# Three more gate/up blocks by seven products, and 22 sums of w_down quarters made by transfers in DRAM

## The chip, the cores and the metric

One core of a Trainium2 chip runs the whole kernel. The metric is the device time in microseconds, the median of the runs. TensorE (PE) multiplies, VectorE (DVE) and ScalarE (ACT) prepare operands and take results, SyncE (SP) issues most transfers, GpSimd (POOL) issues a few and computes some square roots.

## The reference

One layer on x of 512 tokens by 1024 columns, in float32. Everything up to the second residual sum stays as it is; what matters here is its last part, with a hidden width of 2816, that is 22 blocks of 128 columns:

```
h = rms_norm(x, ffn_norm)
a, b = jnp.split(h @ w_gate_up, 2, axis=-1)      # 1024 x (2*2816)
x = x + (jax.nn.silu(a) * b) @ w_down            # 2816 x 1024
return rms_norm(x, final_norm)
```

## The kernel before

**Two-part arithmetic.** A float32 product is made of three products in the format float32r. Each operand is split into a high part (a cast on ACT, "hi") and a low part (source minus high part, a subtraction on DVE, "lo"). So each tile of weights costs PE three matmuls, ACT one cast and DVE one subtraction. The order is counted by semaphores: w_hi and w_lo count split weight parts, used counts the parts that PE is done with. Each engine works its list in the written order.

**Stages.** norm, front, pair (four head pairs), mix, rounds (ten), out, ffn_first, ffn_head, turns, ffn_last, down. The last four make the feed-forward part. Blocks 0 to 3 belong to ffn_first and ffn_head. The fifteen turns (v = 0 to 14) make blocks 4 to 18, each gate and up block by a Strassen-like scheme with seven products of half size: the parts F11, F21, F2, F1, F3, F22, F4 (lines 367 to 370), each 12 matmuls 256 columns wide (`turn_product`, L1346 to L1350). DVE forms four sums of weight quarters per turn (`turn_sums`, `turn_last_sum`), subtracts low parts (`turn_lo`, L2823), adds bank results (`turn_post`, L2831) and multiplies gate with up (`turn_hidden`, L2839). The stage ffn_last makes blocks 19 to 21 plainly: 48 matmuls of 512 columns per block (`whole`, L913 to L917), with `scaled` on DVE and `silu` on ACT.

**Hidden tiles.** Two blocks make one tile r (0 to 10). `hid_sum(r)` is three DVE instructions (L2709, L2714, L2717), then `hidden_hi` (ACT, L1832) and `hid_low` (DVE, L2723) split it. SUMMED is the order in which tiles come. In ffn_last tiles 0, 1, 9 and 10 are handled.

**down.** The product with w_down is also a seven-product scheme in four passes over the eleven tiles: PE's units are two times three matmuls of 512 columns (`both`, `times`, L1400 to L1402). Pass 1 takes two units per tile, from parts NU + 2r and NU + 2r + 1, where NU is the number of parts before this stage. Part NU + 2r is a quarter of w_down as loaded; part NU + 2r + 1 is a sum of two quarters, made on DVE by `first_sum` (L2676) into chain(r). Pass 2 takes three units per tile, with two more sums (`second_sums`, L2926, L2927). Split parts live in a ring of nine places. `down_hi(r)` and `down_lo(r)` or `parts_lo` (L2668) fill it. The high parts of the tile for pass 2 come from `second_hi` (ACT, L1848) and `second_lo` (DVE, L2888). ACT loads another activation table (L1979) between `down_hi(2)` and `down_hi(3)`.

**Transfers.** SP loads 256 KB pieces into `raw`, a store with three slots, each load held back by a wait on w_lo. In ffn_last it also brings back the four 512 KB pages of the second residual (x2_kept, L777), which DVE adds to after pass 1. POOL issues 16 small transfers in the stage pair (L880, L882), and its next work is a square root near 436 us.

Of the kernel before, what the change touches and what calls it, by code (L numbers as in the profile page):

```python
# [36 lines left out]
          ("ffn_first", 1, 2), ("ffn_head", 1, 6), ("turns", 1, 105),  # L37
          ("ffn_last", 1, 6), ("down", 1, 77)]
# [7 lines left out]
TURNS = range(4, 19)  # L46
PER_TURN = 7
TURN_LOADS = 2 * len(TURNS)
LAST_STAGES = ("ffn_last", "down")
# [4 lines left out]
    "free0": dict(front=1, pair=2, mix=1, out=4, ffn_head=1, ffn_last=1),  # L54
    "free1": dict(front=1, pair=2, mix=1, out=3, ffn_first=1, ffn_head=1, ffn_last=1),
    "free2": dict(front=1, pair=1, mix=1, out=4, ffn_head=1, ffn_last=1),
    "free3": dict(front=1, pair=5, mix=1, out=4, ffn_head=1, ffn_last=1),
    "free4": dict(front=2, pair=4, mix=2, out=2, ffn_head=1, ffn_last=1),
    "free5": dict(front=3, pair=4, mix=1, out=2, ffn_head=1, ffn_last=1),
# [20 lines left out]
    "vector_step": dict(norm=11, front=23, pair=5, mix=6, rounds=8, ffn_first=3, ffn_head=5, turns=7, ffn_last=4,  # L80
# [40 lines left out]
def hybrid_block(nc, x, attn_norm, w_in, b_forget, b_gate, w_proj_attn, pool_w, pool_scale,  # L121
# [26 lines left out]
    with ExitStack() as ctx:  # L148
# [36 lines left out]
        w_sums = nc.dram_tensor("w_sums", [16 * P, D // 2], F32, kind="Internal").ap()  # L185
        x2_kept = nc.dram_tensor("x2_kept", [S, D], F32, kind="Internal").ap()
# [125 lines left out]
        def chain(r, n=1):  # L312

            if r == 0:
                return DIAG
            if r < 3:
                return flat[:, (r - 1) * S:(r - 1 + n) * S]
            return early_32[:, (r - 3) * S:(r - 3 + n) * S]

        def in_one(u, n):  # L320

            at = (u - NU) % RING
            if n == 2 and at in (2 * SLOTS - 1, RING - 1):
                return ((0, 1), (1, 1))
            return ((0, n),)

        def ring_part(buf, u, n=1):

            at = (u - NU) % RING * S
            if at >= 2 * SLOTS * S:  # L330
                at += (2 if buf is whi else 5) * S
                return operands[:, at:at + n * S]
            return buf[:].rearrange("p s c -> p (s c)")[:, at:at + n * S]
# [42 lines left out]
        SUMMED = list(TILES.values()) + [0, 1, 9, 10]  # L376
# [116 lines left out]

        def down_raw(k, half, n=1):
# [62 lines left out]
        out_summed, sums_kept = sem("out_summed"), sem("sums_kept")  # L557
        mix_summed, mix_hi, mix_lo = sem("mix_summed"), sem("mix_hi"), sem("mix_lo")
# [32 lines left out]
        def _(sp):  # L591
            def load(stage, i, j, halves, width=P):
# [7 lines left out]
                elif stage == "ffn_last" and j < SLOTS:  # L600
                    v, part, sums = ((-2, F22, 3), (-1, F21, 4), (-1, F22, 4))[j]
                    v += len(TURNS)
                    sp.wait_ge(w_lo, turn_part(v, part) + 1)
                    sp.wait_ge(turn_summed, 4 * v + sums)
                    sp.sem_inc(loads_begun, 1)
# [5 lines left out]
                for src, at in halves:  # L611
# [4 lines left out]
                                 ).then_inc(landed[s], 16)  # L616

# [152 lines left out]
            for j in range(3):  # L770
                for n, c in enumerate(gate_up_columns(19 + j)):
                    load("ffn_last", 0, 2 * j + n, c)
                    t = 2 * j + n - 2
                    if t == 0:
                        sp.wait_ge(used, turn_part(len(TURNS) - 1, F22) + 1)
                    if t >= 0:
                        sp.dma_start(big_x[:, t * D:(t + 1) * D], x2_kept[t * P:(t + 1) * P, :]  # L777
                                     ).then_inc(x2_back, 16)


            def load_down(k, blocks):

                signal = spare_in if k == SPARE else landed[k % SLOTS]
                for at, (row, c) in enumerate(blocks):
                    sp.dma_start(down_raw(k, at),
                                 w_down[row * P:(row + 1) * P, c * HALF:(c + 1) * HALF]
                                 ).then_inc(signal, 16)

            for r in range(R):
                if r == SPARE:  # L790
                    sp.wait_ge(used, NU)
                elif r == SPARE + SLOTS:
                    sp.wait_ge(w_lo, NU + 2 * (SPARE - SLOTS) + 2)
                else:
                    sp.wait_ge(w_lo, NU - SLOTS + r + 1 if r < SLOTS else NU + 2 * (r - SLOTS) + 2)
                sp.sem_inc(loads_begun, 1)
                load_down(r, [(2 * r, 1), (2 * r, 0)])
            for r in range(R):
# [3 lines left out]
                load_down(R + r, [(2 * r, 0), (2 * r + 1, 0)])  # L802
            for q, rows in enumerate(ROWS3):
                if q < SLOTS:
                    sp.wait_ge(w_lo, U_2 + 3 * (R + q - SLOTS) + 3)
                else:
                    sp.wait_ge(w_lo, U_3 + ROWS3[q - SLOTS][-1] + 1)
                    sp.wait_ge(summed, 3 * R + ROWS3[q - SLOTS][-1] + 1)
                sp.sem_inc(loads_begun, 1)
                load_down(2 * R + q, [(2 * r + 1, 1) for r in rows])  # L810
# [21 lines left out]
        def _(pool):  # L832
# [38 lines left out]

            pool.wait_ge(f_rows, 4)
            pool.wait_ge(vector_tile, count("vector_tile", "front", 0, 2))
            for i in range(WB):
                if i > 0:
                    pool.wait_ge(full[6], count("full6", "pair", i - 1, 2))
                for a in range(2):
# [5 lines left out]
                                   ).then_inc(f_in, 16)  # L883

# [13 lines left out]
        def _(pe):  # L898
# [489 lines left out]
            gate_up("ffn_last", 0, 0)  # L1388
            pe.wait_ge(turn_gates, 2 * len(TURNS))
            pe.wait_ge(turn_posted, 4 * len(TURNS))  # L1390
            for j in range(1, 3):
                gate_up("ffn_last", 0, j)

# [24 lines left out]
            for r in range(R):  # L1418
                pe.wait_ge(hid_lo, SUMMED.index(r) + 1)
                both(AB, hid(r, A11 + 2), hid(r, A11), NU + 2 * r, r)  # L1420
                both(DB_, hid(r, S1_ + 2), hid(r, S1_), NU + 2 * r + 1, r)
# [33 lines left out]
        def _(act):  # L1455
            def split_hi(stage, i, j):
# [5 lines left out]
                elif stage == "ffn_last" and j < SLOTS:  # L1462
                    act.wait_ge(used, turn_part(len(TURNS) - 1, (F1, F22, F4)[j]) + 1)
# [344 lines left out]
            def parts_hi(u, src, n=1):  # L1808

                if u < NU + 2 * SLOTS:  # L1810
                    act.wait_ge(used, NU - SLOTS + (u - NU) // 2 + 1)
# [4 lines left out]
            def down_hi(r):  # L1816
# [3 lines left out]
                act.wait_ge(summed, r + 1)  # L1820
# [23 lines left out]
            def second_hi(r):  # L1844

                act.wait_ge(used, NU + 2 * r + 2 if r >= 2 else NU - 4)
# [80 lines left out]
            for v in range(len(TURNS)):  # L1927
# [17 lines left out]
                else:  # L1945
                    split_hi("ffn_last", 0, 0)
# [6 lines left out]
            split_hi("ffn_last", 0, 2)  # L1953
            hidden_hi(0)
            hidden_hi(1)
            wait_free(act, 1, "ffn_head", 0, 1)
            silu("ffn_last", 0)
            split_hi("ffn_last", 0, 3)
            hidden_hi(9)
            split_hi("ffn_last", 0, 4)  # L1960
            wait_free(act, 3, "ffn_last", 0, 1)
            silu("ffn_last", 1)
            split_hi("ffn_last", 0, 5)
            second_hi(0)
            down_hi(0)
            wait_free(act, 5, "ffn_last", 0, 1)
            silu("ffn_last", 2)
            second_hi(1)
            down_hi(1)
            hidden_hi(R - 1)  # L1970
            down_hi(2)
# [12 lines left out]
            for r in range(R):  # L1984
                u, s = U_2 + 3 * r, (R + r) % SLOTS
                act.wait_ge(summed, R + 2 * r + 1)
                parts_hi(u, raw[:, s, 0:2 * HALF], 2)
                act.wait_ge(summed, R + 2 * r + 2)
# [20 lines left out]
            for rows in ROWS4:  # L2009
                act.wait_ge(summed, 3 * R + rows[-1] + 1)  # L2010
# [45 lines left out]
        def _(dve):  # L2056
# [18 lines left out]
            def split_lo(stage, i, j):  # L2075
                n, s = unit(stage, i, j)
                dve.wait_ge(w_hi, n + 1)
                nc.vector.tensor_tensor(wlo[:, s, :], raw[:, s, :], whi[:, s, :].bitcast(F32),  # L2078
# [592 lines left out]
            def first_sum(r):  # L2671

                dve.wait_ge(*landed_down(r))
                if r == 3:
                    dve.wait_ge(used, NU)
                nc.vector.tensor_tensor(chain(r), down_raw(r, 0), down_raw(r, 1),  # L2676
                                        ALU.add).then_inc(summed, 1)

# [173 lines left out]
            for v, block in enumerate(TURNS):  # L2852
                last = v == len(TURNS) - 1
                g, u = GATES_AT[v % 2], UPS_AT[v % 2]
                if v > 0:
# [17 lines left out]
                if last:  # L2873
                    split_lo("ffn_last", 0, 1)
                else:
                    turn_lo(v + 1, F2, turn_sum(0, 2), 2)
# [5 lines left out]
            turn_hidden(len(TURNS) - 1)  # L2882
            split_lo("ffn_last", 0, 2)
# [7 lines left out]
            enter("ffn_last")  # L2891
            hid_sum(0)
            wait_free(dve, 1, "ffn_head", 0, 1)
            hid_sum(1)
            hid_low(0)
            hid_low(1)
            scaled("ffn_last", 0, 19)
            split_lo("ffn_last", 0, 3)
            split_lo("ffn_last", 0, 4)
            hid_low(9)  # L2900
            split_lo("ffn_last", 0, 5)
            first_sum(0)
            scaled("ffn_last", 1, 20)
            down_lo(0)
            first_sum(1)
            second_lo(0)
            first_sum(2)
            down_lo(1)
            second_lo(1)
            scaled("ffn_last", 2, 21)  # L2910
            down_lo(2)
            hid_low(R - 1)
# [7 lines left out]
            def second_sums(r):  # L2920
# [4 lines left out]
                b12, b22 = raw[:, s, 0:HALF], raw[:, s, HALF:2 * HALF]  # L2925
                nc.vector.tensor_tensor(b12, b12, b22, ALU.add).then_inc(summed, 1)  # L2926
# [37 lines left out]
            first_sum(3)  # L2964
            for r in range(3, R):
                parts_lo(NU + 2 * r, down_raw(r, 0))
                if r + 1 < R:
                    first_sum(r + 1)
                else:
# [162 lines left out]
```

## Time and profile before

| | us |
|---|---|
| median of 3 runs (770.55 to 770.76) | 770.66 |
| profiled execution, own time | 770.3 |
| its span | 768.5 |
| PE busy | 759.5 (99%) |
| DVE busy | 649.4 (85%) |
| ACT busy | 420.7 (55%) |
| POOL busy | 18.3 (2%) |
| DMA, share of 16 engines on the SP queue | 42.4% |

Instruction times overlap by their pipeline: the distance from one start to the next is what one instruction costs an engine that has the next one ready. "L913" is a line of the kernel file. A turn is named by v, and its tile by r.

### The profile page before, as it was taken

Reading aid. Unit: us, or ns where it says so; the run is one execution under the profiler, and the core shown is the slowest. Engines: PE = TensorE matmul, PEld = TensorE weight load, DVE = VectorE, ACT = ScalarE, POOL = GpSimd, SP = SyncE. Lnnn points to the kernel's source line nnn. Section 1 sums busy time; section 2 is a strip of 40 time slices with the busy share of each in tenths; the row PEclk is TensorE's granted clock in tenths of the full one; section 3 lists DMA queues with packets and bytes.
Section 4 is the critical chain, followed back from the end, with each engine's and each line's share of the span. In section 5 each row is a group of like instructions: output and inputs, shape, how many; then the busy total and the mean of one; then the engine's idle time right before and its main releaser. Section 6 shows DMA issues by size and latency. Waiting matters only on the chain.

```text
span 768.5 us, 12215 instructions
## 1 busy us (share of the span) xinstructions
PE 759.5 (99%) x4451; PEld 675.3 (88%) x4451; DVE 649.4 (85%) x1041; ACT 420.7 (55%) x712; POOL 18.3 (2%) x41
## 2 busy tenths in 40 slices
PE   8999999999999999999999999999999999999997
PEld 7888888888889999999988888999999998888885
DVE  7788976767798969777787899899999985899997
ACT  6536556646544646555455745555555552655554
POOL 2001100100000000000000000000000000000001
PEclk9999999999999999999999999999999999999999
DMA  8963542324133443344376533333333364443423
GB/s 301 306 202 82 166 111 56 84 55 110 46 93 83 111 127 93 83 110 113 107 269 197 192 111 94 103 106 110 110 101 98 106 209 147 141 161 133 149 89 110
DMA packets 133311, 99.46 MB, mean 129 GB/s; under 512 B 5932, under 2 KB 114532, under 8 KB 133252
## 3 DMA queue, kind: packets, MB, share of 16 engines
q1 hardware_dynamic: 132596, 98.35, 42.4%
q8 instruction: 36, 0.59, 0.3%
q10 hardware_dynamic: 144, 0.26, 0.1%
q14 instruction: 23, 0.19, 0.1%
q0 software_dynamic: 512, 0.07, 0.1%
HBM read 90.21 MB, written 8.39 MB: 128 GB/s over the span
## 4 chain that ended last, share of the span: by engine, by line
PE 98%; DMA 0%; issue 0%; ACT 0%; DVE 0%; POOL 0%; POOLq 0%; DVEq 0%
PE bank L917 10%; PE bank L913 10%; PE bank L915 10%; PE bank L1350 7%; PE bank L1348 7%; PE bank L1346 7%; PE bank L1161 4%; PE bank L1400 4%; PE bank L1159 4%; PE bank L1401 4%; PE bank L1402 4%; PE bank L1157 4%; PE bank L1195 2%; PE bank L1196 2%; PE bank L1197 2%; PE bank L1258 2%
## 5 line engine op out<-in xcount | busy, mean ns | idle before, releaser
L913 PE MATMUL bank<-operands,whi 128*128 128x512 f32 x352 | 137.9, 392 | 0.0
L917 PE MATMUL bank<-operands,wlo 128*128 128x512 f32 x352 | 137.1, 390 | 0.0
L915 PE MATMUL bank<-operands,whi 128*128 128x512 f32 x352 | 137.0, 389 | 0.0
L2078 DVE TENSOR_TENSOR wlo<-raw,whi 128x1024 fp32r<-128x1024 f32 x61 | 74.2, 1223 | 16.8 <-ACT whi L1466 16.0
L1466 ACT CAST whi<-raw 128x1024 fp32r<-128x1024 f32 x61 | 64.1, 1050 | 26.4 <-PE bank L917 7.6
L917 PEld LDWEIGHTS bank<-operands,wlo 128*128 128x128 f32 x352 | 66.1, 188 | 13.9
L915 PEld LDWEIGHTS bank<-operands,whi 128*128 128x128 f32 x352 | 66.1, 188 | 13.3
L913 PEld LDWEIGHTS bank<-operands,whi 128*128 128x128 f32 x352 | 66.1, 188 | 13.3
L1346 PE MATMUL bank<-sums_hi,whi 128*128 128x256 f32 x240 | 67.9, 283 | 0.0
L1348 PE MATMUL bank<-sums_lo,whi 128*128 128x256 f32 x240 | 67.9, 283 | 0.0
L1350 PE MATMUL bank<-sums_hi,wlo 128*128 128x256 f32 x240 | 67.9, 283 | 0.0
L1348 PE MATMUL bank<-operands,whi 128*128 128x256 f32 x180 | 50.9, 283 | 0.0
L1350 PE MATMUL bank<-operands,wlo 128*128 128x256 f32 x180 | 50.9, 283 | 0.0
L1346 PE MATMUL bank<-operands,whi 128*128 128x256 f32 x180 | 50.9, 283 | 0.0
L1346 PEld LDWEIGHTS bank<-sums_hi,whi 128*128 128x128 f32 x240 | 46.1, 192 | 0.0
L1348 PEld LDWEIGHTS bank<-sums_lo,whi 128*128 128x128 f32 x240 | 46.1, 192 | 0.0
L1350 PEld LDWEIGHTS bank<-sums_hi,wlo 128*128 128x128 f32 x240 | 46.1, 192 | 0.0
L1161 PE MATMUL bank<-sums_hi,wlo 128*128 128x256 f32 x160 | 45.3, 283 | 0.0
L1159 PE MATMUL bank<-sums_lo,whi 128*128 128x256 f32 x160 | 45.3, 283 | 0.0
L1157 PE MATMUL bank<-sums_hi,whi 128*128 128x256 f32 x160 | 45.2, 283 | 0.0
L2421 DVE TENSOR_TENSOR wlo<-raw,whi 128x1024 fp32r<-128x1024 f32 (+1 forms) x40 | 38.1, 952 | 3.2 <-ACT whi L1652 3.2
L2823 DVE TENSOR_TENSOR wlo<-raw,whi 128x1024 fp32r<-128x1024 f32 x30 | 36.6, 1220 | 4.1 <-ACT whi L1893 4.1
(323 smaller groups left out, 1995.9 us busy)
## 6 DMA issues: line engine op xcount, KB each, us to landing
raw<-in_w_in_dram SPq DMA_DIRECT2D x105, 256.0 KB, 3.3
raw<-in_w_gate_up_dram SPq DMA_DIRECT2D x88, 256.0 KB, 3.3
raw<-in_w_down_dram SPq DMA_DIRECT2D x53, 256.0 KB, 3.0
big_x<-in_x_dram SPq DMA_DIRECT2D x8, 512.0 KB, 5.3
tiles<-in_w_out_dram SPq DMA_DIRECT2D x4, 1024.0 KB, 7.2
w_sums<-tiles SPq DMA_DIRECT2D x4, 1024.0 KB, 7.2
raw<-w_sums SPq DMA_DIRECT2D x16, 256.0 KB, 3.1
raw<-in_w_out_dram SPq DMA_DIRECT2D x12, 256.0 KB, 3.5
```

The costliest lines, as they stand in the source:

```text
L913: nc.tensor.matmul(banks[b][:, 0:width], whi[:, s, w], op(hi + k * S), start=a, stop=False)
L915: nc.tensor.matmul(banks[b][:, 0:width], whi[:, s, w], op(lo + k * S), start=False, stop=False)
L917: mm = nc.tensor.matmul(banks[b][:, 0:width], wlo[:, s, w], op(hi + k * S), start=False, stop=z)
L1157: nc.tensor.matmul(to, wh[:, w], xh, start=first and k == 0, stop=False, skip_group_check=not first)
L1159: nc.tensor.matmul(to, wh[:, w], xl, start=False, stop=False, skip_group_check=not first)
L1161: mm = nc.tensor.matmul(to, wl[:, w], xh, start=False, stop=k == 3, skip_group_check=not first)
L1346: nc.tensor.matmul(to, wh[:, w], xh, start=first and k == 0, stop=False, skip_group_check=not first)
L1348: nc.tensor.matmul(to, wh[:, w], xl, start=False, stop=False, skip_group_check=not first)
L1350: mm = nc.tensor.matmul(to, wl[:, w], xh, start=False, stop=k == 3, skip_group_check=not first)
L1466: nc.scalar.copy(whi[:, s, :], raw[:, s, :]).then_inc(w_hi, 1)
L2078: nc.vector.tensor_tensor(wlo[:, s, :], raw[:, s, :], whi[:, s, :].bitcast(F32), ALU.subtract).then_inc(w_lo, 1)
L2421: nc.vector.tensor_tensor(part_at(wlo, r, j, n), src, part_at(whi, r, j, n).bitcast(F32), ALU.subtract).then_inc(w_lo, n)
```

## The change

Three things are done at once.

1. TURNS runs to block 21, so there are 18 turns (v = 0 to 17), and the stage ffn_last is gone. down follows the last turn. What ffn_last did for tiles 0, 1 and 10 and for the first three loads of down is written into the last turn and behind it. Tile 9 becomes a tile of the turns.
2. The 22 sums of quarters that used the left or right half of even rows of w_down are formed in DRAM, in a new tensor down_sums of 1408 by 512 values for each kind: POOL copies one quarter there and adds another with an accumulating transfer, from its place in the stage pair. `first_sum` and the first half of `second_sums` leave DVE. SP loads chain(r) and the summed quarter from down_sums, with as many bytes as before.
3. The reload of x2_kept moves from ffn_last to behind the loads 6 to 9 of down. chain(0) moves to a work slot, and the ring of split parts is turned so that it begins behind the last turn's parts.

```diff
-TURNS = range(4, 19)
+TURNS = range(4, 22)
...
+            sp.wait_ge(down_added, 32)
             for r in range(R):
-                if r == SPARE:
+                if r == SLOTS:
                     sp.wait_ge(used, NU)
-                elif r == SPARE + SLOTS:
+                elif r == 1:
+                    sp.wait_ge(w_lo, turn_part(LAST_TURN, F1) + 1)
+                if r == SPARE + SLOTS:
                     sp.wait_ge(w_lo, NU + 2 * (SPARE - SLOTS) + 2)
...
-                load_down(r, [(2 * r, 1), (2 * r, 0)])
+                load_down(r, [(down_block(2 * r, 1), down_raw(r, 0)),
+                              (down_sum(0)[r * P:(r + 1) * P, :], chain(r))])
+                if SPARE <= r < SPARE + TB:
+                    t = r - SPARE
+                    sp.dma_start(big_x[:, t * D:(t + 1) * D], x2_kept[t * P:(t + 1) * P, :]
+                                 ).then_inc(x2_back, 16)
...
+            def copy_down(kind):
+
+                c = 1 - kind
+                pool.dma_start(summed_rows(kind), down[:, :, 0, c * HALF:(c + 1) * HALF]
+                               ).then_inc(down_copied, 16)
+
+            def add_down(kind):
+
+                pool.wait_ge(down_copied, 16 * (kind + 1))
+                pool.dma_start(summed_rows(kind), down[:, :, kind, 0:HALF], accum_op=ALU.add
+                               ).then_inc(down_added, 16)
...
+                if i == 2:
+                    copy_down(0)
+                elif i == 3:
+                    add_down(0)
+                    copy_down(1)
+                    add_down(1)
```

PE: the three `gate_up("ffn_last", ...)` go, and the two waits for the last gate and the last posts move behind the first unit of down.

ACT, from the last turn on:

```diff
                 else:
-                    split_hi("ffn_last", 0, 0)
+                    down_hi(0)
+                    hidden_hi(0)
                 turn_keep(v, F3, right(u))
...
-                    split_hi("ffn_last", 0, 1)
+                    down_hi(1)
             turn_last_gate(len(TURNS) - 1)
...
             hidden_hi(1)
...
+            down_hi(2)
             second_hi(0)
...
+            hidden_hi(R - 1)
+            act.wait_ge(turn_hid, len(TURNS))
             second_hi(1)
-            down_hi(1)
-            hidden_hi(R - 1)
-            down_hi(2)
```

DVE, in the last turn and behind it:

```diff
-                if v > 0:
+                if v > 0 and not last:
                     turn_hidden(v - 1)
...
+                else:
+                    hid_sum(0)
                 dve.wait_ge(used, turn_part(v, F1) + 1)
                 turn_post(v, 2, 2, 2, u, 0)
                 if last:
-                    split_lo("ffn_last", 0, 0)
+                    down_lo(0)
                 turn_post(v, 3, 3, 2, u, 1)
...
+                    hid_low(0)
+                    wait_free(dve, 1, "ffn_head", 0, 1)
+                    hid_sum(1)
                 dve.wait_ge(used, turn_part(v, F22) + 1)
...
                 turn_post(v, 4, 3, 1, u, 0)
...
+            parts_lo(NU + 2, down_raw(1, 0))
+            hid_low(1)
+            parts_lo(NU + 3, chain(1))
+            down_lo(2)
+            for v in range(LAST_TURN - 1, len(TURNS)):
+                turn_hidden(v)
+            dve.wait_ge(turn_hid, len(TURNS))
+            hid_sum(R - 1)
...
             second_lo(0)
+            hid_low(R - 1)
             second_lo(1)
```

Behind that, DVE's loop over r = 3 to 10 is the same without its first_sum.

## Rows read from the trace of the kernel before

**Rows 1.** The page, part 1: busy time, share of the span, instructions.

```profile
PE 759.5 (99%) x4451; PEld 675.3 (88%) x4451; DVE 649.4 (85%) x1041; ACT 420.7 (55%) x712; POOL 18.3 (2%) x41
```

**Rows 2.** Waits of PE, whole span, longest first: total, times, longest.

```profile
PE bank L937 <- POOL ident L837: 2.4, 1, 2.4
...
```

**Rows 3.** Windows: length, then PE, PEld, DVE, ACT, POOL busy; PEclk, DMA share, GB/s.

```profile
474.04:625.23 151.19, 151.19 (x1261) 151.19 (x1260) 139.89 (x220) 84.06 (x141) 0.00 (x0) 1.00 0.37 106
625.23:657.90 32.67, 32.67 (x147) 27.03 (x145) 21.00 (x31) 11.35 (x17) 0.00 (x0) 1.00 0.56 182
625.23:636.12 10.89, 10.89 (x50) 9.01 (x49) 7.90 (x13) 4.00 (x6) 0.00 (x0) 1.00 1.02 329
657.90:758.70 100.80, 100.80 (x446) 83.49 (x445) 98.16 (x140) 59.71 (x91) 1.60 (x2) 1.00 0.38 126
```

**Rows 4.** Timeline of PE (start, length): first matmuls of turns, ffn_last, down.

```profile
474.04 0.28 PE L1346 MATMUL bank<-operands,whi 128*128 128x256 f32 x1
...
625.23 0.40 PE L913 MATMUL bank<-operands,whi 128*128 128x512 f32 x1
...
657.90 0.39 PE L1400 MATMUL bank<-whi,operands 128*128 128x512 f32 x1
```

**Rows 5.** Timeline of DVE at the start of turn 13: turn_lo, turn_post, hid_low.

```profile
605.68 1.21 DVE L2823 TENSOR_TENSOR wlo<-flat,whi 128x1024 fp32r<-128x1024 f32 x1
606.81 0.41 DVE L2831 TENSOR_TENSOR work<-bank,work 128x256 f32<-128x256 f32 x1
607.15 0.68 DVE L2723 TENSOR_TENSOR operands<-tiles,operands 128x512 fp32r<-128x512 f32 x1
607.75 0.68 DVE L2839 SCALAR_TENSOR_TENSOR tiles<-work 128x512 f32<-128x512 f32 x1
```

**Rows 6.** Timeline of DVE: one hid_sum up to the next, later a second_lo.

```profile
628.94 0.69 DVE L2709 TENSOR_TENSOR tiles<-tiles 128x512 f32<-128x512 f32 x1
...
630.46 0.68 DVE L2709 TENSOR_TENSOR tiles<-tiles 128x512 f32<-128x512 f32 x1
...
649.74 0.95 DVE L2888 TENSOR_TENSOR operands<-tiles,high 128x768 fp32r<-128x768 f32 x1
650.61 0.69 DVE L2676 TENSOR_TENSOR flat<-raw 128x512 f32<-128x512 f32 x1
```

**Rows 7.** Timeline of ACT: a second_hi, the table load and the cast behind it.

```profile
643.27 0.84 ACT L1848 CAST high<-tiles 128x768 fp32r<-128x768 f32 x1
...
661.30 1.28 ACT L1979 ACT_TABLE_LOAD   x1
662.59 0.62 ACT L1814 CAST operands<-raw 128x512 fp32r<-128x512 f32 x1
```

**Rows 8.** Timeline of DVE: the low part NU + 6, which tile 3 of down needs.

```profile
663.24 0.69 DVE L2668 TENSOR_TENSOR operands<-raw,operands 128x512 fp32r<-128x512 f32 x1
```

**Rows 9.** Timeline: a load on SP, and the cast on ACT that reads it.

```profile
208.87 0.37 SPq L615 DMA_DIRECT2D raw<-in_w_proj_attn_dram  x1
...
216.92 1.04 ACT L1466 CAST whi<-raw 128x1024 fp32r<-128x1024 f32 x1
```

**Rows 10.** Timeline of POOL: the last of its four transfers in head pair 3.

```profile
151.08 0.58 POOL L882 DMA_DIRECT2D operands<-big_y  x1
```

**Rows 11.** The page, part 3: POOL's queue, with packets and MB.

```profile
q0 software_dynamic: 512, 0.07, 0.1%
```

**Rows 12.** The chain that ended last: PE's attention logits of head pair 3.

```profile
192.76 1.09 PE bank L1102 x10
```

**Rows 13.** Windows, columns as in Rows 3: two stretches with light and medium DMA.

```profile
150.00:185.00 35.00, 35.00 (x175) 29.61 (x174) 25.80 (x57) 21.27 (x47) 1.66 (x4) 1.00 0.29 76
...
670.00:675.00 5.00, 5.00 (x24) 4.14 (x23) 4.98 (x8) 3.86 (x6) 0.00 (x0) 1.00 0.63 209
```

**Rows 14.** The page, part 6: a kind of load, count, size, median us to landing.

```profile
raw<-in_w_down_dram SPq DMA_DIRECT2D x53, 256.0 KB, 3.0
```

More of the change, by code:

```diff
@@ L36 @@
           ("out", 1, 14),
-          ("ffn_first", 1, 2), ("ffn_head", 1, 6), ("turns", 1, 105),
-          ("ffn_last", 1, 6), ("down", 1, 77)]
+          ("ffn_first", 1, 2), ("ffn_head", 1, 6), ("turns", 1, 126),
+          ("down", 1, 77)]
 ROUNDS = [(0, 2)] + [(i, br) for i in range(1, 4) for br in range(3)]
@@ L44 @@
 LATER = ("out", "ffn_first", "ffn_head", "turns")
-TURNS = range(4, 19)
+TURNS = range(4, 22)
 PER_TURN = 7
 TURN_LOADS = 2 * len(TURNS)
-LAST_STAGES = ("ffn_last", "down")
+LAST_STAGES = ("down",)
 RAISED = {
[L54 to L59, printed above, removed]
+    "free0": dict(front=1, pair=2, mix=1, out=4, ffn_head=1),
+    "free1": dict(front=1, pair=2, mix=1, out=3, ffn_first=1, ffn_head=1),
+    "free2": dict(front=1, pair=1, mix=1, out=4, ffn_head=1),
+    "free3": dict(front=1, pair=5, mix=1, out=4, ffn_head=1),
+    "free4": dict(front=2, pair=4, mix=2, out=2, ffn_head=1),
+    "free5": dict(front=3, pair=4, mix=1, out=2, ffn_head=1),
     "free6": dict(front=2, pair=4, mix=1, out=2, ffn_first=1),
@@ L78 @@
     "v_lo_part": dict(pair=2),
-    "vector_step": dict(norm=11, front=23, pair=5, mix=6, rounds=8, ffn_first=3, ffn_head=5, turns=7, ffn_last=4,
+    "vector_step": dict(norm=11, front=23, pair=5, mix=6, rounds=8, ffn_first=3, ffn_head=5, turns=11,
                         down=3),
@@ L322, in in_one @@
             at = (u - NU) % RING
-            if n == 2 and at in (2 * SLOTS - 1, RING - 1):
+            if n == 2 and at in (0, 2 * SLOTS - 1, RING - 1):
                 return ((0, 1), (1, 1))
@@ L375, in hybrid_block @@
         TILES = {v: TURNS[v - 1] // 2 for v in range(1, len(TURNS)) if TURNS[v - 1] % 2}
-        SUMMED = list(TILES.values()) + [0, 1, 9, 10]
+        SUMMED = list(TILES.values()) + [0, 1, 10]
+        LAST_TURN = len(TURNS) - 1
         def turn_part(v, j):
@@ L599, in load @@
                     sp.sem_inc(loads_begun, 1)
[L600 to L605, printed above, removed]
                 elif not (stage == "front" and n < SLOTS):
@@ L616, in load, with turn_raw_read @@
                                  ).then_inc(landed[s], 16)
+            def turn_raw_read(m):
+                v, part, sums = ((-2, F22, 3), (-1, F21, 4), (-1, F22, 3))[m]
+                v += len(TURNS)
+                sp.wait_ge(w_lo, turn_part(v, part) + 1)
+                sp.wait_ge(turn_summed, 4 * v + sums)
             def columns(w, col):
@@ L769, in _ @@
                                      ).then_inc(landed[s], 16)
[L770 to L778, printed above, removed]
@@ L781, in load_down, with down_block @@
-            def load_down(k, blocks):
+            def down_block(row, c):
+                return w_down[row * P:(row + 1) * P, c * HALF:(c + 1) * HALF]
+            def load_down(k, parts):
                 signal = spare_in if k == SPARE else landed[k % SLOTS]
[L784 to L787, printed above, removed]
+                for src, to in parts:
+                    sp.dma_start(to, src).then_inc(signal, 16)
@@ L807, in _ @@
                     sp.wait_ge(w_lo, U_3 + ROWS3[q - SLOTS][-1] + 1)
-                    sp.wait_ge(summed, 3 * R + ROWS3[q - SLOTS][-1] + 1)
+                    sp.wait_ge(summed, R + ROWS3[q - SLOTS][-1] + 1)
                 sp.sem_inc(loads_begun, 1)
-                load_down(2 * R + q, [(2 * r + 1, 1) for r in rows])
+                load_down(2 * R + q, [(down_block(2 * r + 1, 1), down_raw(2 * R + q, at))
+                                      for at, r in enumerate(rows)])
             sp.wait_ge(used, U_2 + 6)
@@ L870, in _, with summed_rows @@
                 root(t, x1_var, x1_rstd)
+            down = w_down.rearrange("(r e p) c -> p r e c", e=2, p=P)
+            def summed_rows(kind):
+                return down_sum(kind).rearrange("(r p) c -> p r c", p=P)
+            def copy_down(kind):
[6 more added lines that the diff above has]
+                               ).then_inc(down_added, 16)
             pool.wait_ge(f_rows, 4)
@@ L1386, in _ @@
                 turn_product(v, F4, a, rows_of(4, 1), False)
[L1388 to L1392, printed above, removed]
             def times(b, high, low, u, m, first, last, onto=False, piece=(0, HALF)):
@@ L2009, in _ @@
             for rows in ROWS4:
-                act.wait_ge(summed, 3 * R + rows[-1] + 1)
+                act.wait_ge(summed, R + rows[-1] + 1)
                 for at, n in in_one(U_4 + rows[0], len(rows)):
@@ L2870, in _ @@
                 if last:
-                    split_lo("ffn_last", 0, 0)
+                    down_lo(0)
                 turn_post(v, 3, 3, 2, u, 1)
-                if last:
-                    split_lo("ffn_last", 0, 1)
-                else:
-                    turn_lo(v + 1, F2, turn_sum(0, 2), 2)
+                if not last:
+                    turn_lo(v + 1, F2, turn_sum(0, 2), 2)
+                else:
+                    hid_low(0)
+                    wait_free(dve, 1, "ffn_head", 0, 1)
+                    hid_sum(1)
                 dve.wait_ge(used, turn_part(v, F22) + 1)
```

82 lines of the change are left out of this document (23 added, 59 removed).

## The prediction

> **What bounds the kernel now.** I read the page first, then the waits of PE, then windows by stage. PE is busy for 759.5 of the 768.5 us [rows 1], and the longest of the waits found for it is 2.4 us at the very start [rows 2]. So the time is PE's own work, and an edit elsewhere counts only where it lets PE wait. By stage [rows 3], PE is busy for the whole of the turns (151.19 us), of ffn_last (32.67) and of down up to its last matmuls (100.80), always at a granted clock of 1.00. The reader should look at DVE in the same rows: 139.89 of 151.19 in the turns is 93%, 21.00 of 32.67 in ffn_last is 64%, and 98.16 of 100.80 in down is 97%. ffn_last is a stage in which DVE has slack, between two in which it has almost none. The change removes that stage.
>
> **PE's work.** The fifteen turns run from 474.04 to 625.23, so one costs 151.19 / 15 = 10.079 us; ffn_last takes 657.90 - 625.23 = 32.67 us for three blocks [rows 4]. Three more turns cost 30.24. The saving is **2.43 us**. down would begin at 474.04 + 18 x 10.079 = 655.47. Its 12 matmuls per tile in pass 1 stay, and at ffn_last's 32.67 / 144 = 0.227 us each they are 2.72 us per tile. The two waits moved behind the first unit of down (last gate, last posts) must end by 655.47 + 1.36 = 656.83.
>
> **The new turns inside.** Turns 15 and 16 have the lists of every earlier turn, in which PE did not wait [rows 2, 3]: no cost. Turn 17 gives up the four sums for a next turn and takes hid_sum(0), down_lo(0), hid_low(0) and hid_sum(1).
>
> **The joint between the last turn and down.** This is where ffn_last's cover is gone, so I add up DVE's list. Costs are from start to next start: a 1024-wide subtraction 1.13 us, a 256-wide post 0.34, a 512-wide instruction 0.60 [rows 5]; a hid_sum 630.46 - 628.94 = 1.52 and a second_lo 650.61 - 649.74 = 0.87 [rows 6]. Turn 13 starts at 474.04 + 13 x 10.079 = 605.07, and its first post stands 1.74 us later, at 606.81 [rows 5]. Turn 17 follows a turn with a hid_sum as 13 does, so the same post stands at 645.39 + 1.74 = 647.13. From there to the low part NU + 6, the first that tile 3 of down needs, the new list holds five posts (1.70), one 1024-wide subtraction (1.13), thirteen 512-wide instructions (hid_low of 9, 0, 1 and 10; lo of F4; six low parts of tiles 0 to 2; two turn_hidden: 7.80), three hid_sums (4.56) and two second_lo (1.74): 16.93 us. The last turn's final post comes after the first 8.9 of these, at 656.0, which is 0.8 before PE asks for it. The parts of tiles 1 and 2 are ready at 657.8 and 659.1, ahead of 658.2 (its first unit, which needs only the earlier half) and 660.9. NU + 6 then begins at 647.13 + 16.93 = 664.06 and takes 0.69 [rows 8]: 664.75.
>
> ACT gives the same date. Its hidden_hi(10) waits for the first instruction of hid_sum(10), which ends after 13.07 + 0.69 us of DVE's list, at 660.9. Behind it stand one 512-wide cast (0.62), second_hi(1) (0.84), the table load (1.29 to the next start) and the cast of NU + 6 (0.62) [rows 7]: 664.3, then 0.69 on DVE, 664.95.
>
> PE wants it at 655.47 + 3 x 2.72 = 663.63. So PE **waits 1.1 to 1.3 us at tile 3**; I take 1.2, since both chains agree. Before, the same part was done at 663.24 + 0.69 = 663.93 [rows 8] for a need at 657.90 + 8.16 = 666.06, 2.1 us early. Behind the stall DVE needs 1.2 us per tile against PE's 2.72 and draws ahead, since the first_sums are gone. Bounds: 0, if both lists run 1.2 us shorter than added up; 2.4, double, if the handoffs between ACT and DVE add 0.1 us each in a list with some ten of them.
>
> **The sums.** Eleven first_sums and eleven half second_sums leave DVE: 22 x 0.60 = 13.2 us, of 98.16 in down [rows 3, 5]. PE did not wait for DVE there, so this gives PE nothing by itself; it pays for the catching up.
>
> **POOL's transfers.** Each copy moves 1408 x 512 x 4 B = 2.88 MB; at the 329 GB/s of a full stretch [rows 3] that is 8.8 us. The adding ones are not in the trace; they read twice, so between 8.8 and some 26 us each. POOL's own issue: 0.54 us for a transfer of 512 / 16 = 32 packets [rows 10, 11] is at most 17 ns each, so 1408 rows take at most 24 us. The first copy starts near 117 us. The rest starts behind POOL's last small transfer of pair 3, 151.08 + 0.58 = 151.66 [rows 10], and takes from 26 to some 96 us, so it ends between 178 and 248. Queued behind them on POOL is only the square root near 436 us. Pair 3's small transfers stand behind the first copy: they have until PE's logits at 192.76 [rows 12]. SP asks for the sums near 640. What could be hit is SP's loads, which share the engines: the DMA share is 0.29 at 150 to 185 [rows 13]. The load with least room there is issued at 208.87 and its cast starts at 216.92 [rows 9], 8 us for a 512 KB that needs 1.6 us at full rate. I count **0**; bounds 0 and 1 us (a load in the first rounds).
>
> A rule that speaks against this stands in the Trainium skill, "SBUF — State Buffer", in the part on two separate sides: while DVE runs certain two-port instructions GpSimd can't write descriptors, and its transfers starve. No row of before shows a long POOL transfer beside DVE. By that rule the four would be late, but they have some 390 us of room, so the sum stays the same.
>
> **The pages of x2.** 2 MB leave the stretch after 624 us and come in behind loads 6 to 9, from about 659 and 667 on. From 667.6 to the sum for pass 2, SP issues five loads of 512 KB and three pages: 4.19 MB, 12.7 us at 329 GB/s, plus 2.2 us to land (estimated from the 3.0 us of a 256 KB load [rows 14], less 0.8 for its bytes): 682.5. Pass 1's last low part stands behind the second_sums(0) that wants it, which must start by 684.2 if PE is late by 1.2. Cost **0**, with 1.7 us to spare.
>
> **The sum.** Against the profiled execution: 768.5 - 2.43 + 1.2 = 767.3 span, 769.1 with the 1.8 us around it. The median of the runs lies 0.36 above that execution: **769.5**. All the tail behind PE stays.
>
> **The rivals.**
> *A, no stall* (20%): ACT and DVE arrive in time at tile 3. Then all of the 2.43 us stays, 768.2. For it: the lists are tight, a start 1.2 us earlier is enough. Against it: DVE's 93% in the turns.
> *B, slower through the transfers* (14%): the moved pages crowd the loads of pass 1. The 4.19 MB would have to take over 684.2 - 667.6 - 2.2 = 14.4 us, that is run below 291 GB/s; at the 209 GB/s of a busy stretch of down [rows 13] they take 20.0 and PE waits 5.6 us more: 775.1. For it: the pages and the loads are in one queue, in order. Against it: 329 GB/s in the very stretch in which pages and loads met before [rows 3]; the 209 is asked for, not the limit, its DMA share being 0.63.
> *C, a partial form* (10%): the stall at tile 3 is 2.4 us, so that nothing is left: 770.7.
>
> **How the numbers follow.** A measurement of this kernel can tell about 0.2%, 1.5 us, from no change. My own case (56%) has 1.2 us gained, between 768.9 and 770.3, nearly all of it "same"; C is "same" as well; A is "faster"; B is "slower". With a tenth of my case, the part below 769.1, put to faster: faster 0.26, same 0.60, slower 0.14. The range reaches from just under A's 768.2, at 767.9, through C up to 772.5, where B's waits up to 3 us lie.
>
> **What would show it.** The first matmul of down at 655.5 and 84 matmuls per turn at the same pace (PE's work). A wait of PE of 1.1 to 1.3 us near 663.6, on the low part L2668 of NU + 6, with the table load just before it on ACT (the joint). No wait of PE between 117 and 260 us (POOL). No wait of DVE for a load near 681 to 684 (pages); one there means B. The forecast falls if down is already late at its first tile, if PE waits in the rounds, or if the stall is elsewhere than at tile 3.

## The result, and the profile after

The changed kernel takes **774.74 us** (774.34 to 775.26, 4 runs) against 770.71 before (770.55 to 770.83, 4 runs): ratio 1.0053, 95% interval 1.0035 to 1.007. It is slower by 4.0 us. The forecast was 769.5, with 767.9 to 772.5 as its range. The profiled execution took 774.65 us, its span is 772.8 and its mean granted clock 0.996.

The page, part 1 (busy time, share, instructions), and parts of 3 and 6, against [rows 1, 11]:

```profile
PE 759.4 (98%) x4559; PEld 679.5 (88%) x4559; DVE 653.6 (85%) x1050; ACT 428.4 (55%) x731; POOL 24.5 (3%) x45
...
q0 software_dynamic: 4800, 11.60, 6.4%
...
down_sums<-in_w_down_dram POOLq DMA_DIRECT2D x4, 2816.0 KB, 21.0
```

PE's busy time is what it was, although 2.4 us of work is gone: matmuls at a lower clock count as busy for longer, as is seen below. So the loss is waiting and slow running, not work. The waits of PE, whole span (what, for whom, total, times, longest), against [rows 2]:

```profile
PE bank L975 <- POOL ident L851: 2.4, 1, 2.4
PE bank L1125 <- DVE stat L2312: 2.3, 1, 2.3
PE bank L1432 <- DVE operands L2689: 1.4, 1, 1.4
PE bank L978 <- ACT big_y L1528: 1.2, 1, 1.2
```

The third is the wait at tile 3 of down that the prediction named. The second is new, and it stands at 185 us, in head pair 3, 475 us ahead of that joint. The chain that ended last shows how it comes about (start, length, what):

```profile
165.85 0.37 SPq L617
166.26 16.48 DMA raw<-in_w_in_dram
182.77 1.05 ACT whi L1499
183.84 1.22 DVE wlo L2098
185.10 0.29 DVE big_y L2312
185.46 0.38 PE bank L1125
```

A load of weights took 16.5 us to land. ACT had the cast next in its list, DVE had the subtraction ahead of the masked logits, and those are what frees a bank for PE's second set of logits. The timeline of PE there:

```profile
182.75 0.40 PE L955 MATMUL bank<-operands,wlo 128*128 128x512 f32 x1
185.46 0.38 PE L1125 MATMUL bank<-operands 128*128 128x256 f32 x1 [2.31 <-DVE stat L2312]
...
187.94 0.63 PE L951 MATMUL bank<-operands,whi 128*128 128x512 f32 x1
188.37 0.63 PE L953 MATMUL bank<-operands,whi 128*128 128x512 f32 x1
...
189.22 0.58 PE L951 MATMUL bank<-operands,whi 128*128 128x512 f32 x1
189.63 0.40 PE L953 MATMUL bank<-operands,whi 128*128 128x512 f32 x1
189.87 0.40 PE L955 MATMUL bank<-operands,wlo 128*128 128x512 f32 x1
```

From 187.1 to 189.6 a matmul of 512 columns comes every 0.43 us, before the gap and from 189.6 on every 0.23. The granted clock of 186.3 to 189.6 is 0.50 (windows below): that is the lower of TensorE's two levels, 1.2 GHz and not 2.4, after 2.7 us between one matmul's start and the next. So the wait has a second price. In the kernel before, the same stretch is (timeline of PE):

```profile
182.14 0.39 PE L917 MATMUL bank<-operands,wlo 128*128 128x512 f32 x1
182.37 0.28 PE L1087 MATMUL bank<-operands 128*128 128x256 f32 x1
...
184.88 0.39 PE L917 MATMUL bank<-operands,wlo 128*128 128x512 f32 x1
```

Up to 182.75 the changed execution is 0.61 us behind; at 185.46 it is 3.09 behind 182.37; at 189.87 it is 4.99 behind 184.88. So the **wait costs 2.48 and the slow stretch 1.90 us**. The turns begin at 479.06 and not 474.04, 5.02 later. From there the turns go as forecast, and the joint costs 0.4 us more than was forecast. The span was forecast at 767.3 and is 772.8: of these 5.5 us the wait and the slow stretch are 4.4, the joint is 0.4, and 0.6 was lost at the very start of this execution.

Windows (length, then PE, PEld, DVE, ACT, POOL busy; PEclk, DMA share, GB/s), against [rows 3]:

```profile
479.06:660.50 181.44, 181.44 (x1514) 181.43 (x1512) 170.44 (x270) 101.19 (x172) 0.00 (x0) 1.00 0.36 105
660.50:762.90 102.40, 101.00 (x447) 83.31 (x446) 92.00 (x130) 61.53 (x96) 1.59 (x2) 1.00 0.46 152
184.00:190.00 6.00, 4.54 (x14) 3.59 (x15) 5.34 (x22) 2.80 (x10) 0.47 (x1) 0.72 1.00 174
186.30:189.60 3.30, 3.30 (x9) 2.66 (x9) 2.71 (x13) 2.40 (x9) 0.00 (x0) 0.50 1.09 193
158.00:163.00 5.00, 5.00 (x34) 4.36 (x33) 2.46 (x6) 3.76 (x9) 0.00 (x0) 1.00 1.12 210
```

Eighteen turns take 181.44 us, 10.08 each. The last row is a stretch in which POOL's adding transfer moves: the DMA engines are full and move 210 GB/s, where [rows 3] has 329.

POOL, timeline, against [rows 10]:

```profile
151.68 0.57 POOL L914 DMA_DIRECT2D operands<-big_y  x1
152.25 2.04 POOL L901 DMA_DIRECT2D down_sums<-in_w_down_dram  x1
153.41 1.96 POOL L895 DMA_DIRECT2D down_sums<-in_w_down_dram  x1
182.61 1.87 POOL L901 DMA_DIRECT2D down_sums<-in_w_down_dram  x1 [27.23 <-DMA down_sums<-in_w_down_dram]
```

The first addition and the second copy go out 1.2 us apart. The time to landing of each is 12.3 us for the first copy at 117, 21.1 for the first addition, 28.9 for the copy behind it and 20.9 for the second addition. POOL's wait before the last row ends when that copy has landed, at 182.3. That is where the late load lands too.

Why it lands there is seen in the packets of the two queues, POOL's (q0) and SP's (q1), with packets, MB and share, in 160 to 164, in 174 to 180 and in 180 to 182.7 (DMA view):

```profile
q0 software_dynamic: 332, 0.68, 91.3%
q1 hardware_dynamic: 327, 0.17, 20.9%
...
q0 software_dynamic: 493, 2.02, 87.5%
q1 hardware_dynamic: 492, 0.24, 15.8%
...
q1 hardware_dynamic: 1072, 0.53, 74.5%
q0 software_dynamic: 74, 0.24, 23.3%
```

While both queues have work they move the same number of packets, but POOL's hold 2 KB in the addition and 4 KB in the copy, and SP's 512 B. So SP's queue gets some 82 packets a us, and 397 once POOL's has run out. A load of 512 KB is 1024 such packets, some 12.5 us at 82 a us (an estimate from these rows). The load ahead of the late one, issued at 155, landed only by 172.6, so the late one will have had little before that (the rows don't tell one load's packets from the other's). POOL's two transfers also go one behind the other: up to 164 its packets are all 2 KB, from 174 on all 4 KB.

### The profile page after: what moved, and what is told of

Same layout as the page of the kernel before. It is cut to its first block, busy times and chain, and to the rows that moved or that the text cites. A ratio compares the mean times of both kernels' runs of the same rounds, so it can differ in the third digit from the quotient of the medians.

```text
span 772.8 us, 12500 instructions
## 1 busy us (share of the span) xinstructions
PE 759.4 (98%) x4559; PEld 679.5 (88%) x4559; DVE 653.6 (85%) x1050; ACT 428.4 (55%) x731; POOL 24.5 (3%) x45
## 4 chain that ended last, share of the span: by engine, by line
PE 93%; DMA 3%; DVE 2%; ACT 1%; issue 1%; POOL 0%; POOLq 0%; SPq 0%; DVEq 0%; ACTq 0%
PE bank L951 8%; PE bank L953 8%; PE bank L955 8%; PE bank L1388 8%; PE bank L1386 8%; PE bank L1384 8%; PE bank L1199 4%; PE bank L1197 4%; PE bank L1195 4%; PE bank L1432 4%; PE bank L1433 4%; PE bank L1434 4%; PE bank L1233 2%; PE bank L1234 2%; PE bank L1235 2%; DMA raw<-in_w_in_dram 2%
## 5 line engine op out<-in xcount | busy, mean ns | idle before, releaser
L951 PE MATMUL bank<-operands,whi 128*128 128x512 f32 x304 | 119.7, 394 | 0.0
L955 PE MATMUL bank<-operands,wlo 128*128 128x512 f32 x304 | 118.7, 390 | 0.0
L953 PE MATMUL bank<-operands,whi 128*128 128x512 f32 x304 | 118.6, 390 | 0.0
L1384 PE MATMUL bank<-sums_hi,whi 128*128 128x256 f32 x288 | 81.5, 283 | 0.0
L1386 PE MATMUL bank<-sums_lo,whi 128*128 128x256 f32 x288 | 81.5, 283 | 0.0
L1388 PE MATMUL bank<-sums_hi,wlo 128*128 128x256 f32 x288 | 81.5, 283 | 0.0
L951 PEld LDWEIGHTS bank<-operands,whi 128*128 128x128 f32 x304 | 57.4, 189 | 11.6
L953 PEld LDWEIGHTS bank<-operands,whi 128*128 128x128 f32 x304 | 57.4, 189 | 11.6
L1386 PE MATMUL bank<-operands,whi 128*128 128x256 f32 x216 | 61.1, 283 | 0.0
L1388 PE MATMUL bank<-operands,wlo 128*128 128x256 f32 x216 | 61.1, 283 | 0.0
L1384 PE MATMUL bank<-operands,whi 128*128 128x256 f32 x216 | 61.1, 283 | 0.0
L1386 PEld LDWEIGHTS bank<-sums_lo,whi 128*128 128x128 f32 x288 | 55.3, 192 | 0.0
L1199 PE MATMUL bank<-sums_hi,wlo 128*128 128x256 f32 x160 | 45.3, 283 | 0.0
L1197 PE MATMUL bank<-sums_lo,whi 128*128 128x256 f32 x160 | 45.3, 283 | 0.0
L1195 PE MATMUL bank<-sums_hi,whi 128*128 128x256 f32 x160 | 45.2, 283 | 0.0
L1941 ACT COPY work<-bank 128x256 f32<-128x256 f32 x54 | 20.1, 373 | 43.8 <-PE bank L1388 43.6
```

Of the source, the lines that this page charges most:

```text
L951: nc.tensor.matmul(banks[b][:, 0:width], whi[:, s, w], op(hi + k * S), start=a, stop=False)
L953: nc.tensor.matmul(banks[b][:, 0:width], whi[:, s, w], op(lo + k * S), start=False, stop=False)
L955: mm = nc.tensor.matmul(banks[b][:, 0:width], wlo[:, s, w], op(hi + k * S), start=False, stop=z)
L1195: nc.tensor.matmul(to, wh[:, w], xh, start=first and k == 0, stop=False, skip_group_check=not first)
L1197: nc.tensor.matmul(to, wh[:, w], xl, start=False, stop=False, skip_group_check=not first)
L1199: mm = nc.tensor.matmul(to, wl[:, w], xh, start=False, stop=k == 3, skip_group_check=not first)
```

## The experiments

The theory at this point, T: POOL's transfers in pair 3 hold up the load that SP issues at 166 us, and the joint gains 0.8 us. The rival J: the loss belongs to the joint and the moved work.

**b_transfers**: the transfers alone, in the kernel before, where nothing reads their sums.

```diff
+                if i == 2:
+                    copy_down(0)
+                elif i == 3:
+                    add_down(0)
+                    copy_down(1)
+                    add_down(1)
...
+            pool.wait_ge(down_added, 32)
             pool.wait_ge(norm_var, 1)
```

> The kernel before with the four transfers of POOL added in the same places (head pairs 2 and 3) and nothing that reads them. Theory T (the transfers hold up SP's loads in pair 3, PE waits 2.3 us at 185 us and then runs some us at the lower clock level): 775.2, that is 4.5 us over before, with the first logits of pair 3 late as in the changed kernel. Rival J (the loss comes from the joint between the last turn and down): 770.7, no change.

775.67 us (774.7 to 777.74), ratio to before 1.006, interval 1.0041 to 1.0079. The longest wait of PE (waits of b_transfers):

```profile
PE bank L1118 <- DVE stat L2322: 3.0, 1, 3.0
```

The transfers by themselves cost all of the loss and 0.8 us more, which is what the rest of the change gives back in a_quarters below. J is out.

**a_quarters**: the changed kernel without the transfers.

```diff
-            sp.wait_ge(down_added, 32)
...
-                              (down_sum(0)[r * P:(r + 1) * P, :], chain(r))])
+                              (down_block(2 * r, 0), chain(r))])
...
-                load_down(R + r, [(down_sum(1)[r * P:(r + 1) * P, :], down_raw(R + r, 0)),
+                load_down(R + r, [(down_block(2 * r, 0), down_raw(R + r, 0)),
...
```

(the lines that issue POOL's four transfers go too; SP loads plain quarters, so this kernel leaves the sums out and computes something else in the same time pattern)

> The changed kernel without POOL's four transfers: SP loads one plain quarter of w_down wherever it loaded a sum, so the output is not the reference's; all else is the same. Theory T: the joint alone is left, 2.4 us of PE's work saved and 1.6 us waited at tile 3 of down, so 769.9; up to 770.5 if the 0.6 us by which the changed kernel was already late at 16 us stays. Rival J: 774.7 as the changed kernel.

770.01 us (769.76 to 771.91) beside 770.83 for before, ratio 0.999, interval 0.9981 to 0.9999: 0.8 faster. Of the waits of the changed kernel the one at tile 3 is there, the one at 185 is not (waits of a_quarters):

```profile
PE bank L1407 <- DVE operands L2664: 1.4, 1, 1.4
```

The two parts of the change are apart now: the turns with their joint give 0.8 us, the transfers take 4.7 to 4.8.

**a_one_by_one**: never more than one transfer of POOL in flight.

```diff
                     add_down(0)
+                    pool.wait_ge(down_added, 16)
                     copy_down(1)
```

> The changed kernel, but the second copy waits until the first addition has landed, so never more than one transfer of POOL is in flight. If it is the two at once (issued at 152 and 153 us) that hold up the load issued at 166 us: its landing falls from 16 us to 10 or less and the time to 770 to 771. If a single adding transfer takes as much of the engines: the wait at 185 us stays, 774 to 775.

770.02 us (769.74 to 771.34), ratio 0.9984, interval 0.9975 to 0.9994. One wait on an engine that has nothing else to do takes back 4.7 us. The time from issue to landing for the two loads issued in 164 to 168, in the changed kernel and then here:

```profile
DMA to landing us min/median/max: 13.9/15.2/16.5
```

```profile
DMA to landing us min/median/max: 7.8/8.1/8.3
```

The addition is here waited for until 173.6, and the load issued at 166.2 lands at 174.5. So a single addition holds the load up as well, but it ends before the cast needs the load (180.0 here). The wait gives SP's queue, between the addition and the second copy, a stretch of its own in which it catches up: 661 packets in 172 to 173.5.

**b_one_by_one**: the same wait, in the kernel before with the transfers (the edit is shown against b_transfers).

```diff
                 elif i == 3:
                     add_down(0)
+                    pool.wait_ge(down_added, 16)
                     copy_down(1)
```

> The kernel before with the four transfers, additions too, but the second copy issued only when the first addition has landed. Theory T with the two in flight as the cause: no wait of PE at 185 us, 770.7, no change against before. If 22 sums by transfer cost something of their own even so: 771.5 or more.

770.9 us (770.54 to 771.42), ratio 0.9999, interval 0.999 to 1.0008. So the four transfers, issued in this way, cost nothing that the interval can tell. The 22 sums are still on DVE in this kernel, so it says nothing of what taking them off DVE is worth.

**b_copies**: the four transfers in their first places, two at once, but plain (the edit is shown against b_transfers).

```diff
-                pool.dma_start(summed_rows(kind), down[:, :, kind, 0:HALF], accum_op=ALU.add
+                pool.dma_start(summed_rows(kind), down[:, :, kind, 0:HALF]
                                ).then_inc(down_added, 16)
```

> The kernel before with POOL's four transfers in the first places (two issued at once at 152 us), but all four plain copies, no addition. Theory A (an adding transfer is slow and holds SP's loads, a copy takes 12 us): load issued at 165 us lands in 10 us or less, no wait of PE, 770.7. Rival V (any such transfer holds them up): the wait of 2 to 3 us stays, 775.

771.13 us (770.62 to 772.45), ratio 1.0005, interval 0.9996 to 1.0014, and no wait of PE at the logits. POOL's timeline and the landing of the loads issued in 164 to 168:

```profile
153.58 1.08 POOL L887 DMA_DIRECT2D down_sums<-in_w_down_dram  x1
175.93 1.05 POOL L893 DMA_DIRECT2D down_sums<-in_w_down_dram  x1 [21.26 <-DMA down_sums<-in_w_down_dram]
```

```profile
DMA to landing us min/median/max: 9.6/10.5/11.4
```

The expectation of theory A was 10 us or less, so it is only nearly right: copies hold loads up too. The pair of copies is through at 176, the addition with the copy at 182.3, and the load follows them, by 178 and at 182.7. Its cast starts at 179.8 here and at 182.8 in the changed kernel: a part of the difference is taken up by the load's room, the other 3 us are ACT's wait, which PE's follows.

**a_small_rows**: are 512 B rows of POOL kinder to 512 B rows of SP?

```diff
-                pool.dma_start(summed_rows(kind), down[:, :, kind, 0:HALF], accum_op=ALU.add
-                               ).then_inc(down_added, 16)
+                for q in range(4):
+                    at = slice(q * P, (q + 1) * P)
+                    pool.dma_start(summed_rows(kind)[:, :, at], down[:, :, kind, at],
+                                   accum_op=ALU.add).then_inc(down_added, 16)
```

(and the copies in the same way, with the waits counted up to match)

> The changed kernel with each of the four transfers cut into four of 128 columns, so that its rows are 512 B as those of SP's loads and not 2 KB; same bytes, same places. Theory P (a DMA engine takes turns between the queues by the packet, so SP's 512 B rows get a small share beside 2 KB rows): the loads of pair 3 land in some 7 us, not 14 to 17, PE waits under 1 us there, 770 to 771. Theory V (only the volume counts, the engines are full): landing 14 to 17 us as before the cut, 774.7. If 512 B rows make the transfers themselves much longer, loads of mix come into reach too and the time may rise over 774.7.

772.9 us (772.26 to 774.61), ratio 1.0025, interval 1.0016 to 1.0035: between the two. The loads issued in 164 to 168 land in 8.8 us (median), while the copies are still under way until 190.9; so they no longer land with POOL's end. While both queues move, each has some 200 packets of 512 B a us (796 and 771 in 170 to 174) and SP's queue gets half of the bytes, where it had a fifth beside the addition. That is theory P, though its time of 770 to 771 is missed. The transfers last 8.6 us longer, the loads issued in 173 to 177 need 13.1, and PE waits 1.7 us elsewhere. The timelines there, POOL, ACT, then DVE:

```profile
190.86 7.72 POOL L906 DMA_DIRECT2D down_sums<-in_w_down_dram  x4 [8.35 <-DMA down_sums<-in_w_down_dram]
```

```profile
190.81 1.05 ACT L1504 CAST whi<-raw 128x1024 fp32r<-128x1024 f32 x1 [3.71 <-DMA raw<-in_w_in_dram]
```

```profile
191.89 1.23 DVE L2103 TENSOR_TENSOR wlo<-raw,whi 128x1024 fp32r<-128x1024 f32 x1 [3.88 <-ACT whi L1504]
194.30 2.63 DVE L2333 TENSOR_SCALAR big_y<-big_y,stat 128x128 f32<-128x128 f32 x4
196.85 1.67 DVE L2111 TENSOR_TENSOR operands<-bank,operands 128x512 fp32r<-128x512 f32 x4
```

A load is late again, and four multiplications on DVE take 2.63 us while POOL issues; more on that below.

**a_act_early and a_both_early**: the joint. Both are a_one_by_one with ACT's list changed, the second with DVE's too.

```diff
             second_hi(0)
+            down_hi(3)
...
-            for r in range(3, R):
+            for r in range(4, R):
                 down_hi(r)
```

```diff
             hid_sum(R - 1)
+            parts_lo(NU + 6, down_raw(3, 0))
+            parts_lo(NU + 7, chain(3))
...
-            for r in range(3, R):
+            for r in range(4, R):
                 parts_lo(NU + 2 * r, down_raw(r, 0))
```

> The kernel a_one_by_one with only ACT's list reordered, DVE's as it is. If both lists gave tile 3 the same date, as the prediction had it, the low part starts 0.2 us sooner at most, PE still waits 1.2 to 1.4 us, 769.9. If ACT with its table load is what held the part up: no wait, 768.6.

770.0 us (769.52 to 771.61), ratio 0.999, interval 0.9981 to 0.9999: the same as a_one_by_one. PE's wait and DVE's list in front of the part (waits, then timeline, of a_act_early):

```profile
PE bank L1433 <- DVE operands L2691: 1.2, 1, 1.2
```

```profile
662.32 0.95 DVE L2913 TENSOR_TENSOR operands<-tiles,high 128x768 fp32r<-128x768 f32 x1
663.19 0.68 DVE L2738 TENSOR_TENSOR last_tile<-last_tile,last_tile 128x512 fp32r<-128x512 f32 x1
663.79 0.95 DVE L2913 TENSOR_TENSOR operands<-tiles,high 128x768 fp32r<-128x768 f32 x1
664.66 0.69 DVE L2691 TENSOR_TENSOR operands<-raw,operands 128x512 fp32r<-128x512 f32 x1
```

ACT now casts the part at 659.8, almost 5 us ahead, and DVE comes to it no sooner than its list allows. 2.34 us of work for pass 2 and tile 10 stands in front of it. PE's wait is 1.2 us where a_one_by_one has 1.4, as expected.

> The kernel a_one_by_one with both lists reordered at the joint: ACT casts the parts of tile 3 before hidden_hi(10) and the table load, DVE subtracts their low parts right behind hid_sum(10), before the two second_lo. Theory D (tile 3 waits for the list of DVE, 2.4 us of other work stands ahead of its part): no wait of PE at tile 3, 770.0 - 1.5 = 768.5, and against before -2.3 us. Rival F (the wait is paid back elsewhere, at tile 4 or in pass 2): 769.5 to 770.

**768.63 us** (767.98 to 771.07), ratio to before 0.9974, interval 0.9965 to 0.9983. It beats both kernels, before by 2.2 us and the changed one by 6.1. The part comes straight behind hid_sum(10) (timeline of DVE), and the only wait of PE left in its list of waits is the one at the very start:

```profile
662.03 0.42 DVE L2732 SCALAR_TENSOR_TENSOR last_tile<-last_tile 128x256 f32<-128x256 f32 x1
662.37 0.68 DVE L2691 TENSOR_TENSOR operands<-raw,operands 128x512 fp32r<-128x512 f32 x1
```

Rival F is out: nothing was paid back at tile 4 or in pass 2.

## Why the prediction was wrong, step by step

**PE's work, 2.43 us saved: right.** Fifteen turns of 10.079 became eighteen of 10.08, and with both waits taken away the gain is 2.2 us.

**The joint, 1.2 us lost: right in place and cause, 0.4 too small.** down begins at 660.50 and tile 3 could start 8.16 later, at 668.66; it starts at 670.25, so 1.6. DVE subtracted the part from 669.41 on; forecast, moved by the 5.02 us of the turns' later start, was 669.08. Both lists ended together, as added up (ACT, then DVE, timelines of after):

```profile
668.76 0.62 ACT L1847 CAST operands<-raw 128x512 fp32r<-128x512 f32 x1
```

```profile
669.41 0.69 DVE L2689 TENSOR_TENSOR operands<-raw,operands 128x512 fp32r<-128x512 f32 x1
```

ACT's cast ended at 669.38 and DVE's own list was through at about 669.2. So neither list alone was the one to mend: with ACT's alone (a_act_early) 0.2 us of the wait went, with both (a_both_early) all of it. DVE's alone was not run; with the cast at its old date the part could hardly have come sooner.

**22 sums off DVE, worth nothing by itself: it fits, but no run shows it alone.** Turns and joint as measured, 2.43 gained and 1.6 lost, make 0.8, which is all that a_quarters and a_one_by_one gain.

**The pages of x2, 0: right.** ACT waited up to 1.9 us for single loads of down_sums in pass 1, and PE did not.

**POOL's transfers, "I count 0; bounds 0 and 1 us": this is the step that failed**, with 4.7 to 4.8 us in its place, and in three ways.
- *The price of a load.* It said "8 us for a 512 KB that needs 1.6 us at full rate". That is the load's bytes alone on idle engines. Beside POOL's transfers a load shares the engines packet by packet, 512 B against 2 or 4 KB, and waits behind the load ahead of it: from 3.3 us for its half (before, issued at 165) it went to 10.6 beside one copy at 119 and to 15.2 beside addition and copy. The transfers' own times were within the bounds taken (12.3 for a copy where 8.8 was expected, 21 for an addition out of 8.8 to 26), and so was their end, 203.5; the issue of one, bounded at 24 us, took 1.1 to 2.0. Only what they do to a neighbour was priced as if they weren't there.
- *The load with least room.* The one at 208.87 [rows 9] was after they had ended. The one hit had 13.8 us of room in the kernel before (issued at 165.25, cast at 179.02). Least room over a stretch was the wrong question; right was to ask, for every load beside the transfers, what its room is against its landing there. This one landed 16.5 us after its issue.
- *What a stall costs.* A wait of PE was priced at its own length. The delay of 2.5 us brought 1.9 more at the lower clock. The 1.8 us gap at tile 3 did not: the granted clock stayed at 1.00 behind it, and so it did behind the gap of 2.1 us at 195.6 in a_small_rows.

The rival that came out on this side, B, was about slower through transfers, but at another place and for another cause. Its place shows no wait of PE, so it is luck that its 775.1 lies near the 774.74 measured.

**The 0.6 us at the start** is no part of the change: the profiled execution of the changed kernel waited 1.2 us for the first tokens at 8 us, a_quarters, with the same code there, not at all, and before 0.7. With the same code it varies from run to run.

## What to carry to other kernels

Before a large transfer is put "in the background", take it that a load beside it, from another queue and with smaller rows, may land only when the transfer ends, and compare that date with the load's room; and give each large one a wait for the last, since one wait on an idle engine was worth 4.7 us here. Where a stage with slack is removed, write out the list of every engine that feeds the first consumer behind it, and take out of all of them what only a later pass needs: that was 1.4 us here. And look behind a wait of PE for a stretch at half clock: here 2.3 us of waiting brought one, 1.4 and 1.7 us did not.

## What the runs showed of the hardware

- **A queue beside a large transfer of another queue gets packets in equal number, not bytes.** 327 of SP's to 332 of POOL's in 160 to 164, with 0.17 MB against 0.68; beside plain copies (b_copies, same stretch) 255 to 259, with 0.13 against 1.04. The Trainium skill ("DMA: Bandwidth & Descriptors", on queues, rings and completion order) has a DMA engine take turns between queues by the packet; these counts agree. The load issued at 166 lands within 2 us of the end of POOL's transfers: at 182.7 for 182.3 in the changed kernel, 174.5 for 173.6 in a_one_by_one, by 178 for 175.9 in b_copies. With POOL's rows at 512 B it landed in 8.8 us with POOL's still running.
- **Not explained:** beside POOL's transfers SP's first packets come late. The load issued at 155 has its first ones near 159, and the one issued at 166 in a_small_rows near 170, where in the kernel before they come within 2 us.
- **An adding transfer in DRAM** takes 21 us for 2.88 MB where a copy takes 12.3, both beside SP's loads. With the addition the full engines move 211 GB/s (a_one_by_one, 160 to 172), with copies 326 (b_copies, 165 to 175).
- **POOL's issuing slows some of DVE's instructions.** L2333 multiplies four tiles of 128x128 up to 128x512: 1.28 us in a_small_rows at 186.74, with no issue of POOL beside it, 2.63 at 194.30 while POOL issued for 7.72 us. The same instructions took 1.27 in the kernel before at 189.72, and 1.85 in the changed kernel at 151.87, beside an issue of 2.04. The subtraction of the same stretch took its usual 1.23. The rule of the Trainium skill in "SBUF — State Buffer", told ahead of the result, has the starving on GpSimd's side; here it is DVE that was late. That page also says that whichever comes first blocks the other. In a_small_rows POOL's issuing did come first, so the rows agree in who was late; but the four multiplications ended at 196.93 and POOL's four issues at 198.58, so DVE was not held up for the whole of them.
- **The granted clock** was 0.72 on the mean of 184 to 190. Behind the 2.7 us gap it was 0.95 for the first 0.9 us, then 0.50 from 186.3 to 189.6, and 0.99 from there on. In b_transfers, after 3.4 us, it was 0.54 from 186.6 to 190.
